# Split matrix products in passes: all slices high by high, then all high by low, then all low by high

## What is computed

```python
h = rmsnorm(x, g_mix_pre)
q, k, v, u, qx, gates = split(h @ w_in)
y_attn = sliding_window_attention(rope(q), rope(k), v, sinks)      # window 128, 8 heads of 64
y_ssm  = s5_branch(u, ...)                                         # state space, GELU, w_glu
km, vm = split(rmsnorm(mem, g_mem) @ w_mem_kv)                     # 256 memory tokens
y_mem  = memory_cross_attention(qx, km, vm)
gt = sigmoid(gates)                                                # three gates per channel
merged = gt0 * (y_attn @ w_branch_attn) + gt1 * (y_ssm @ w_branch_ssm) + gt2 * (y_mem @ w_branch_mem)
x = x + rmsnorm(merged @ w_out, g_mix_post)
h = rmsnorm(x, g_mlp_pre)
f = square(relu(h @ w_up)) @ w_down                                # 1024 -> 4096 -> 1024
x = x + rmsnorm(f, g_mlp_post)
```

## Time and profile before

| | |
|---|---|
| median of 3 runs | 1585.14 us (1581.22 to 1585.4) |
| profiled execution | 1585.63 us |
| its span, first to last instruction | 1583.8 us |
| mean granted clock of TensorE | 0.994 of full |
| TensorE: matmuls, weight loads | 7403 each, busy 1547.2 and 1297.1 us |
| VectorE, ScalarE, GpSimd busy | 833.4, 460.8, 119.6 us |
| DMA | 130.94 MB, mean 83 GB/s |

### The profile page before, as it was taken

The page is one execution under the profiler, slowest core; times in us unless marked ns, Lnnn a source line. Parts: engine busy times, 40 slices in busy tenths (PEclk is TensorE's granted clock), DMA queues, the critical chain, the costliest instruction groups (busy, mean ns, idle before and its releaser), DMA issues.

```text
span 1583.8 us, 18390 instructions
## 1 busy us (share of the span) xinstructions
PE 1547.2 (98%) x7403; PEld 1297.1 (82%) x7403; DVE 833.4 (53%) x1581; ACT 460.8 (29%) x647; POOL 119.6 (8%) x190
## 2 busy tenths in 40 slices
PE   6899999999999999999999999999999999999997
PEld 5788779878888888888888888888888888888886
DVE  6838658657746725446766643333333333333348
ACT  5443744332222234221343322112130212121132
POOL 2000010041220221100000200000000000000000
PEclk9899999999999999999999999999999999999999
DMA  8301120242112245324432420111101111101104
GB/s 298 88 27 53 41 92 29 87 127 93 67 54 100 60 138 184 131 83 156 145 109 80 146 74 33 54 53 53 53 26 53 53 53 53 51 28 53 53 1 173
DMA packets 82208, 130.94 MB, mean 83 GB/s; under 512 B 13120, under 2 KB 55136, under 8 KB 82144
## 3 DMA queue, kind: packets, MB, share of 16 engines
q1 hardware_dynamic: 66400, 76.03, 14.7%
q0 software_dynamic: 15744, 54.03, 9.9%
HBM read 104.88 MB, written 25.17 MB: 82 GB/s over the span
## 4 chain that ended last, share of the span: by engine, by line
PE 94%; DVE 3%; DMA 2%; issue 1%; ACT 1%; SPq 0%; POOL 0%; DVEq 0%; ACTq 0%
PE bank L1426 87%; PE bank L1439 2%; DMA raw<-in_w_mem_kv_dram 1%; PE bank L1644 1%; PE bank L1531 1%; PE bank L1658 1%; PE bank L1599 1%; PE bank L1627 0%; PE bank L1546 0%; PE bank L1662 0%; DVE wlo L305 0%; DMA tok<-in_x_dram 0%; DVE prob L1000 0%; DVE mx L998 0%; DVE hTlo L933 0%
## 5 line engine op out<-in xcount | busy, mean ns | idle before, releaser
L1426 PE MATMUL bank<-hThi,whi 128*128 128x512 f32 x1184 | 463.7, 392 | 1.2 <-DVE hTlo L933 0.7
L1426 PE MATMUL bank<-hThi,wlo 128*128 128x512 f32 x1184 | 461.7, 390 | 0.0
L1426 PE MATMUL bank<-hTlo,whi 128*128 128x512 f32 x1184 | 461.7, 390 | 0.0
L1426 PEld LDWEIGHTS bank<-hThi,whi 128*128 128x128 f32 x1184 | 222.9, 188 | 48.4 <-issue 2.7
L1426 PEld LDWEIGHTS bank<-hThi,wlo 128*128 128x128 f32 x1184 | 222.8, 188 | 46.7
L1426 PEld LDWEIGHTS bank<-hTlo,whi 128*128 128x128 f32 x1184 | 222.9, 188 | 45.8
L299 ACT ACTIVATE whi<-raw 128x2048 fp32r<-128x2048 f32 x65 | 124.1, 1911 | 377.7 <-PE bank L1426 333.2
L1426 PE MATMUL bank<-whi,yhi 128*128 128x512 f32 x512 | 199.3, 389 | 0.8 <-DVE wlo L305 0.8
L1426 PE MATMUL bank<-whi,ylo 128*128 128x512 f32 x512 | 199.2, 389 | 0.0
L1426 PE MATMUL bank<-wlo,yhi 128*128 128x512 f32 x512 | 199.2, 389 | 0.0
L305 DVE TENSOR_TENSOR wlo<-raw,whi 128x2048 fp32r<-128x2048 f32 x65 | 148.8, 2290 | 70.2 <-ACT whi L299 69.5
(11 more groups left out here) (314 smaller groups left out, 1854.9 us busy)
## 6 DMA issues: line engine op xcount, KB each, us to landing
raw<-in_w_in_dram SPq DMA_DIRECT2D x34, 512.0 KB, 4.6
raw<-in_w_up_dram SPq DMA_DIRECT2D x32, 512.0 KB, 4.3
raw<-in_w_down_dram SPq DMA_DIRECT2D x32, 512.0 KB, 4.3
gate_scratch<-scr POOLq DMA_DIRECT2D x48, 256.0 KB, 2.3
tok<-gate_scratch POOLq DMA_DIRECT2D x24, 512.0 KB, 3.6
raw<-in_w_mem_kv_dram SPq DMA_DIRECT2D x8, 512.0 KB, 8.7
y_scratch<-yst POOLq DMA_DIRECT2D x16, 256.0 KB, 2.5
yst<-y_scratch POOLq DMA_DIRECT2D x16, 256.0 KB, 4.3
```

The lines of the kernel that those rows point to most:

```text
L1426: ins = T.matmul(dst, lhs(k)[p], rhs(k)[q], start=start and k == 0 and i == 0, stop=stop and k == kt - 1 and i == 2)
```

## The change

In `product`, the two loops change places. Before, the three matmuls of a slice stand together; now all slices of one kind stand together: high by high for every k, then high by low, then low by high. The waits of `ready` are made in the first pass. Each product has the same matmuls into the same bank, in another order.

```diff
 def product(dst, lhs, rhs, kt, start=True, stop=True, ready=None):
-    for k in range(kt):
-        if ready:
-            ready(k)
-        for i, (p, q) in enumerate(((0, 0), (0, 1), (1, 0))):
+    for i, (p, q) in enumerate(((0, 0), (0, 1), (1, 0))):
+        for k in range(kt):
+            if ready and i == 0:
+                ready(k)
             ins = T.matmul(dst, lhs(k)[p], rhs(k)[q], start=start and k == 0 and i == 0,
                            stop=stop and k == kt - 1 and i == 2)
     return ins
```

## The result

| | before | after |
|---|---|---|
| median of 15 runs each, side by side | 1582.6 us (1580.47 to 1586.6) | 1585.95 us (1583.54 to 1590.67) |
| profiled execution; its span | 1585.63; 1583.8 us | 1585.93; 1584.2 us |
| matmuls of line 1426 | 6336 | 6336 |

The ratio is 1.0023, with a 95% interval of 1.0015 to 1.003: the medians lie 3.35 us apart, clear of zero and inside the 0.3% that was set as no change. So the two traces are compared place by place, not by their spans.

A forecast was written before the change was run, and what follows sets the result against it. The prediction took TensorE as the bound: number of matmuls times the distance between starts, plus few waits. Its terms 0 + 1.7 + 1.5 = +3.2 us on the median 1585.14 gave 1588.3 us, range 1583.8 to 1591.5.

The forecast's parts named there:

- Distance between starts: Line 1426, all 6336 matmuls: start-to-start distance stays 0.226 us in passes, repeated stationary slices saving nothing; 0 us.
- Queued matmuls: First w_out product: 14 ready matmuls end up queued behind the waits for slices 6 and 7; +1.7 us.
- Clock: Behind the waits of the first w_out product: thin TensorE work brings one half-clock stretch; +1.5 us, bounds 0 and 1.7.
- the stated chance of 0.55: Whole kernel: chance given to the main forecast, the gathered wait in w_out plus one half-clock stretch.
- the first rival: First w_out product: the gathered wait alone, clock stays up; +1.7 us, 1586.8 us; chance 0.25.
- Nothing gives it back: After the first w_out product: no later TensorE wait absorbs the 1.7 us; all engines shift together.
- The sum: Whole kernel: 0 + 1.7 + 1.5 = +3.2 us, giving 1588.3 us, 0.20% slower.
- The second: Behind the w_out waits: clock stays down for two stretches, +4.6 up to +5.1 us, about 1590 us; chance 0.10.
- The third: Every matmul: passes cost or give something, 3 ns each being 19 us (1604 or 1566 us); chance 0.03 each way.
- The fourth: Whole kernel: the change does nothing for the time, TensorE not held up at the eight waits; 1585 us; chance 0.04.

The follow-up runs named there:

- the filled kernel: Against the changed kernel: 14 and 6 extra matmuls into another bank ahead of the waits for slices 6 and 7 in the first w_out product; ratio 1.0014.
- the kernel with one long wait: Against the changed kernel: the first matmul of the first w_out product waits for all eight slices; ratio 1.0023 to before, median 1586.7 us.
- the kernel without waits there: Against before: first two w_out products interlaced, and kinds needing only high halves put ahead of two later waits for low halves of weights; ratio 0.9991, 1580.22 us.
- the last two: Against before: interlaced w_out products with high-half kinds ahead of two low-half waits, 0.9991; the same plus that order at four memory weight units, 0.9985.
- the first experiments: Against before: passes in all products except the first w_out product, ratio 0.9999; passes only in that product, ratio 1.0015.

## Why the prediction was right

*Distance between starts, 0.* Right: 0.226 us before and after, the kernel with passes everywhere else at 0.9999, the one without repeated slices at 1.0006 with an interval that holds 1.

*Queued matmuls, +1.7 us.* Right: 1.67 us in the length with the clock held up. That slice 7 starts when VectorE releases it, whatever TensorE does, held in every kernel that waits there: 4.01 to 4.03 us behind the first start.

*Clock, +1.5 us.* Right in mechanism and, in the profiled execution, in size: one stretch of 3.4 us, wholly under matmuls, 1.50 us by the difference to the filled kernel. That the fall would come was reached by likeness, 0.8 busy of 3.7 us against the stretches ahead of earlier falls, and the profile shows 0.94 of 3.70. The likeness was weaker than it looked: the same first stretch, 0.93 busy of 4.05 us, brought no fall in the profiled execution of the change. So that the fall came here is in part luck, for which the stated chance of 0.55 left room. Both profiled kernels with these two waits showed it, and the mean clocks of the timed runs fit a fall in most of them. The size was taken midway between 1.2 and 1.7 us. The 1.2 rests on a slip: the 18 matmuls of the stretch include two that had started ahead of it, and 16 x 0.12 = 1.9 us from 3.35 is 1.4 to 1.5 us. The medians (3.35 us apart, at least 2.4 by the interval) exclude the first rival, in which it never comes, at 95%.

*Nothing gives it back.* Right: 3.17 us in the place, 3.35 in the medians.

*The sum.* 3.2 us forecast, 3.35 measured, with an interval of 2.4 to 4.7: that they agree to 0.2 us is closer than the runs can show. The absolute 1588.3 us was 2.4 too high: the three runs of before that it was added to had a median of 1585.14, fifteen had 1582.6. The measured 1585.95 lies in the range.

*Rivals.* The second, slower by two stretches, didn't come in the profiled execution of the change; it came in the kernel with one long wait, where 6.8 us at half, all but 1.2 of them under matmuls, cost 2.5 us. 1590.67 us, the slowest run of the change, has the lowest mean clock of its fifteen, 0.991, and may be one, but no profile shows it. The third, a price or gain per matmul, fell in both directions, since passes have the same 0.226 us. The Trainium skill ("TensorE: Matmul & The Clock Gate", "Back-to-back issue gap") gives about 216 ns for 512 columns, as the gap of an isolated matmul, and about 131 ns for a stream of weight loads and matmuls; this case's trace shows neither, and the 0.226 us decides. The excess over the 216 is not a cost of alternating operands; what it is, no run here shows. The fourth was wrong as argued.

## What to carry to other kernels

An order of matmuls into one bank is free only where nothing waits inside it: count the ready instructions that a new order puts behind each wait, since on an in-order queue those are the price (here 24 of 6336 matmuls carried all of it). Where the array would stand nearly still (here 0.94 us busy of 3.70), allow for a half-clock stretch behind it; it cost 1.50 us here, nearly as much as the queued matmuls, though a stretch as thin did not bring one every time. And passes are worth using the other way round: put the kinds that need only early operands ahead of the wait, and leave to the end the kind that needs the late one, then ask which producer is late next.

## What was not expected

**A wait costs more than the list of waits shows.** Before, TensorE's idle time in `w_out` is 1.1 us, but its length is 13.12 us where 11.51 is possible, as the kernel without waits there shows: 1.6 us. The list counts from the end of the last matmul, which is in flight for 0.28 us while its successor could have started after 0.12, and the first start after a wait is followed by a distance of 0.22 instead of 0.12.

**The scatter of the runs goes with the clock of the first 66 us.** All kernels have thin stretches of TensorE there, and in how many the clock falls differs from one execution to the next of nearly the same program. The first 66 us of before, and behind them those of the kernel without repeated slices, which differs in the order of kinds alone (columns as above):

```profile
0.00:66.00 66.00, 43.85 (x288) 41.08 (x289) 50.36 (x101) 36.41 (x57) 9.40 (x23) 0.90 0.70 224
```

Without repeated slices:

```profile
0.00:66.00 66.00, 44.26 (x301) 41.29 (x302) 52.30 (x102) 36.52 (x58) 9.38 (x23) 0.95 0.73 231
```

A mean clock of 0.90 is 13 us at half, one of 0.95 is 7 us. The spans are 1583.8 and 1580.2 us.

The other traces bear this out. Eight profiled kernels (all but the last two) differ up to `w_out` in the order inside products alone. TensorE could start `w_out` at 776.0, 776.0 and 777.3 us in the three that had some 7 us at half in that part, at 776.8, 778.5 and 779.1 in the three with 10, and at 779.6 both times with 13.6. That is about 1.6 us for each stretch of 3.4 us, with more than a microsecond left over between kernels of one group. It also shows in the timed runs of before beside the first experiments: the ten with a mean clock of 0.994 average 1584.7 us, the thirteen with 0.996 average 1582.1. So two spans of one execution each (here 1583.8 and 1584.2) don't measure a change of 3 us, while a length between two fixed instructions does.
